# Attention by feature in a two-block layer kernel, and the recurrence's heads normed and turned by halves

## The reference

```python
proj = rms_norm_2(x, g_pre) @ w_in
q_h, f_h, i_h, z_h, q_a, k_a, v_a, z_a = split(proj)
o_h = hgrn2(q_h, f_h, i_h, lb)                       # gated recurrence, 8 heads of 128
o_h = rms_norm_2(o_h, g_head) * silu(z_h)            # per head
o_a = sliding_window_attention(rotary(q_a), rotary(k_a), v_a, sinks)   # 16 heads of 64, window 128
y = concatenate([o_h, o_a * silu(z_a)]) @ w_out
x = x + rms_norm_2(y, g_post)
```

## Time and profile before

| | us |
|---|---|
| median of 3 runs | 1220.43 |
| the runs | 1215.7, 1220.43, 1221.11 |
| the profiled execution | 1216.97 |
| its span, first to last instruction | 1214.8 |
| TensorE busy in it | 1079.9 (89%) |
| VectorE busy | 838.6 (69%) |
| ScalarE busy | 671.2 (55%) |
| GpSimd busy | 71.1 (6%) |
| mean granted TensorE clock | 0.942 |

### The profile page before, as it was taken

The page is one execution under the profiler, slowest core; times in us unless marked ns, Lnnn a source line. Parts: engine busy times, 40 slices in busy tenths (PEclk is TensorE's granted clock), DMA queues, the critical chain, the costliest instruction groups (busy, mean ns, idle before and its releaser), DMA issues.

```text
span 1214.8 us, 16346 instructions
## 1 busy us (share of the span) xinstructions
PE 1079.9 (89%) x6089; PEld 930.8 (77%) x6089; DVE 838.6 (69%) x1516; ACT 671.2 (55%) x1324; POOL 71.1 (6%) x46
## 2 busy tenths in 40 slices
PE   5789798769599999999988899999887889999887
PEld 4668686668588887787877888888766888888766
DVE  5566553456559999999975866686567766587654
ACT  5345374524378988788854487523335378633233
POOL 0100200000010101003000000100101000010100
PEclk9989798879689999999999999999898999999889
DMA  8522124304149999999964322332243322332220
GB/s 333 173 104 105 57 83 162 115 36 174 36 162 398 348 379 365 351 381 369 388 233 161 134 105 104 139 139 105 88 156 130 144 108 105 143 135 105 88 86 35
DMA packets 30034, 211.44 MB, mean 174 GB/s; under 512 B 3328, under 2 KB 3712, under 8 KB 4992
## 3 DMA queue, kind: packets, MB, share of 16 engines
q1 hardware_dynamic: 28368, 205.01, 45.1%
q10 hardware_dynamic: 1584, 5.34, 1.2%
HBM read 209.28 MB, written 1.05 MB: 173 GB/s over the span
## 4 chain that ended last, share of the span: by engine, by line
PE 59%; DVE 21%; ACT 9%; DMA 5%; issue 4%; POOL 2%; SPq 0%; DVEq 0%; POOLq 0%
PE ps L484 15%; PE ps L486 14%; PE ps L485 14%; DVE w_lo L383 9%; DMA ring<-in_panels 5%; PE ps L489 4%; PE ps L925 3%; ACT s_buf L1737 3%; PE ps L633 2%; ACT L1737 2%; POOL stat L395 2%; DVE gates L383 1%; PE ps L691 1%; DVE scr L383 1%; DVE op_lo L383 1%
## 5 line engine op out<-in xcount | busy, mean ns | idle before, releaser
L383 DVE TENSOR_TENSOR w_lo<-ring,w_hi 128x512 fp32r<-128x512 f32 x760 | 488.4, 700 | 201.0 <-ACT w_hi L1690 200.2
L1690 ACT ACTIVATE w_hi<-ring 128x512 fp32r<-128x512 f32 x760 | 424.8, 620 | 249.5 <-PE ps L486 216.2
L484 PE MATMUL ps<-w_hi,op_hi 128*128 128x512 f32 (+2 forms) x928 | 370.5, 399 | 21.6 <-DVE w_lo L383 13.4
L485 PE MATMUL ps<-w_lo,op_hi 128*128 128x512 f32 (+2 forms) x928 | 361.5, 390 | 0.0
L486 PE MATMUL ps<-w_hi,op_lo 128*128 128x512 f32 (+2 forms) x928 | 361.5, 390 | 0.0
L484 PEld LDWEIGHTS ps<-w_hi,op_hi 128*128 128x128 f32 x928 | 177.9, 192 | 63.3 <-DVE w_lo L383 22.2
L486 PEld LDWEIGHTS ps<-w_hi,op_lo 128*128 128x128 f32 x928 | 177.3, 191 | 36.4
L485 PEld LDWEIGHTS ps<-w_lo,op_hi 128*128 128x128 f32 x928 | 177.9, 192 | 32.0
L484 PE MATMUL ps<-op_hi,w_hi 128*128 128x256 f32 x448 | 134.5, 300 | 8.2 <-DVE op_lo L383 8.2
L485 PE MATMUL ps<-op_lo,w_hi 128*128 128x256 f32 x448 | 130.5, 291 | 0.0
L486 PE MATMUL ps<-op_hi,w_lo 128*128 128x256 f32 x448 | 130.2, 291 | 0.0
(11 more groups left out here) (226 smaller groups left out, 1059.1 us busy)
## 6 DMA issues: line engine op xcount, KB each, us to landing
ring<-in_panels SPq DMA_DIRECT2D x194, 1024.0 KB, 6.4
cst<-in_c ACTq DMA_DIRECT2D x1, 1219.0 KB, 5.3
buf_a<-in_pre ACTq DMA_DIRECT2D x2, 512.0 KB, 6.2
keys<-in_post ACTq DMA_DIRECT2D x2, 512.0 KB, 3.6
out<-x_tok SPq DMA_DIRECT2D x2, 512.0 KB, 2.6
cst<-in_c ACTq DMA_DIRECT2D x1, 960.0 KB, 7.0
x_tok<-in_x SPq DMA_DIRECT2D x1, 512.0 KB, 4.7
x_tok<-in_x ACTq DMA_DIRECT2D x1, 512.0 KB, 4.9
```

The source lines that it names most:

```text
L383: return V.tensor_tensor(o, a, b, op)
L484: T.matmul(o, l[0], r[0], start=start, stop=False)
L485: T.matmul(o, l[0], r[1], start=False, stop=False)
L1690: return A.activation(o, a, ACT.Copy, scale=scale)
```

## The change

- `turn` is no longer a transpose. VectorE (`weigh`, new) makes the reciprocals before it, in the sparse attention times the gate, and writes four diagonal matrices, identity times reciprocal. TensorE multiplies the exponentials by them in six fp32 products. The turned probabilities come out already divided.
- `values` has V as the stationary side, in four products with 256 or 128 columns of tokens, so the output is by feature. In the forgetting attention ScalarE and VectorE split it at once into `fox_hi` and `fox_lo`; in the sparse attention VectorE adds the branches; in the second block VectorE multiplies silu(z_a), which is now projected by feature. `up_turns`, `att_turn` and `att_gate` are gone; `up_split` (behind 43) and `att_split` (behind takes 32 and 33 of a layer) split without a turn.
- VectorE runs `scores_out` and `weigh` ahead of the other small work of a take, right behind the feed.
- The projection of z_a moves from takes 26 to 33 to takes 10 to 17 of a layer, the q and f of the recurrence to 18 to 33; the levels from the second on are one take earlier, `cross` is behind 48 and 49.
- `head_norm`, the new `head_scale` and `hg_turn` go by halves of the heads. Eight small products apply inverse root and gate together; the head gain is applied in the split behind the turns.
- In the first block `fox_norms` is behind take 9, `nsa_sides` behind 26, the sparse jobs start one take later, the compression's products use the weighted probabilities, and its weights are loaded one half panel earlier.

```diff
     def weight_halves():
+            if n == 8 and h == 1:
+                out += [(2 * PN_CMP + i, 0, None) for i in range(2)]
             if n == 9 and h == 0:
-                out += [(2 * PN_CMP + i, 0, None) for i in range(2)]
-            if n == 9 and h == 1:
                 out += [(2 * PN_CMP + 2 + i, 0, None) for i in range(2)]
...
     def at_ticks(table, rows):
-        for name, job in (("values", values), ("turn", turn), ("scores", scores)):
+        for name, job in (("weigh", turn), ("values", values), ("turn", turn), ("scores", scores)):
...
-    table.setdefault(b + 33, []).append(("att_gate", l))
+    for a in range(TT):
+        table.setdefault(b + 32 + a, []).append(("att_split", (l, a)))
     for lv in range(LEVELS):
         for j in range(2):
-            table.setdefault(b + L_IH + 2 * lv + j, []).append(("level", (l, lv, j)))
-    table.setdefault(b + 49, []).extend([("cross", (l, 0)), ("cross", (l, 1)), ("att_turn", l)])
...
+            table.setdefault(b + L_IH + 2 * lv + j - (lv > 0), []).append(("level", (l, lv, j)))
+    for j in range(2):
+        for take, name in ((48, "cross"), (50, "hgrn_values"), (51, "head_norm"), (53, "head_scale"), (54, "hg_turn")):
+            table.setdefault(b + take + j, []).append((name, (l, j)))
...
             def turn(job):
-                pe.wait_ge(score_p, job + 1)
+                pe.wait_ge(weighed, job + 1)
...
-                        m = turn128(ps[:, 4 + e, i * P:(i + 1) * P], s_of(job)[:, e * 384 + c:e * 384 + c + P])
+                        m = T.matmul(ps[:, 4 + e, i * P:(i + 1) * P], s_of(job)[:, e * 384 + c:e * 384 + c + P],
+                                     weight_of(job, 1 if i else 0, e), start=True, stop=True)
...
+            def weigh(job):
+                dve.wait_ge(score_p, job + 1)
+                if job >= L1_JOBS:
+                    dv(tt(sm, sm, ex, ALU.add))
+                    settle()
+                dv(V.reciprocal(rec, sm))
+                settle()
...
+                dve.wait_ge(turn_mm, job)
+                for a in range(TT):
+                    for e in range(2):
+                        m = ts(weight_of(job, a, e), ident[:, :], rec[:, 2 * a + e:2 * a + e + 1], None, ALU.mult)
+                m.then_inc(weighed, 1)
...
             def values(job):
+                for kt in range(2):
+                    for e in range(2):
+                        half, cc = slice(e * HD, (e + 1) * HD), c + e * HD
+                        pt = pt_of(job)[:, e * 384:(e + 1) * 384]
+                        m = T.matmul(ps[half, 6, kt * P:S], v3[:, kt, cc:cc + HD], pt[:, kt * S:S + kt * P],
                                      start=kt == 0, stop=kt == 1)
...
+            def head_scale(arg):
...
+                for a in range(TT):
+                    for h in range(4):
+                        m = V.scalar_tensor_tensor(oh[:, a, h, :], oh[:, a, h, :], ss[:, a, h:h + 1], zh[:, a, h, :],
+                                                   ALU.mult, ALU.mult)
+                m.then_inc(hg_done, 1)
...
+            def ahead(t):
+                feed(2 * t + AHEAD)
+                for name, arg in beside.get(t, ()):
+                    if name in ("weigh", "scores_out"):
+                        table[name](arg)
```

More of the change, by code:

```diff
@@ new lines, in dve_program, with up_split, att_split @@
+            cmp_sums, value_sums = [6], (10, 11)
+            def up_split(_):
+                for r in range(PAIRS):
+                    dve.wait_ge(up_hi, r + 1)
+                    o = operand(1024 + r * S, S)
+                    tt(tm(o[1]), z3[:, :, ZNQ + r * P:ZNQ + (r + 1) * P], tm(o[0].bitcast(F32)),
+                       ALU.subtract).then_inc(up_lo, 1)
+            def att_split(arg):
+                l, a = arg
+                for h in range(2):
+                    dve.wait_ge(split_hi, 4 * l + 2 * a + h + 1)
+                    c = ZQA + h * 512
+                    tt(att_lo[:, a, c:c + 512], zb3[:, a, c:c + 512],
+                       att_hi[:, a * D + h * 512:a * D + (h + 1) * 512].bitcast(F32), ALU.subtract).then_inc(split_lo, 1)
@@ L1602, in dve_program @@
                 which, i = divmod(t - T_UP, 4)
-                if i == 0:
-                    for n in range(2):
-                        dve.wait_ge(up_hi, 2 * which + n + 1)
-                        o = operand(1024 * which + n * 512, 512)
-                        tt(o[1], ps[:, n, :], o[0].bitcast(F32), ALU.subtract).then_inc(up_lo, 1)
-                feed(2 * t + AHEAD)
+                ahead(t)
                 b = i % 2
@@ L1746, in turn_out_, with values_out, up_split, att_split @@
                 copy(pt_of(job).rearrange("p (e c) -> p e c", e=2), ps[:, 4:6, 0:384]).then_inc(turn_out, 1)
+            def values_out(job):
+                if job < FOX_JOBS:
+                    act.wait_ge(value_mm, job + 1)
+                    copy(fox_rows(job)[0], ps[:, 6, 0:S]).then_inc(value_hi, 1)
+            def up_split(_):
+                act.wait_ge(cmp_v, 8)
+                for r in range(PAIRS):
+                    act.wait_ge(value_out, 9 + r)
+                    copy(tm(op_hi[:, 1024 + r * S:1024 + (r + 1) * S]),
+                         z3[:, :, ZNQ + r * P:ZNQ + (r + 1) * P]).then_inc(up_hi, 1)
+            def att_split(arg):
+                l, a = arg
+                act.wait_ge(value_out, L1_JOBS + SWA_PAIRS * (l + 1))
+                for h in range(2):
+                    c = ZQA + h * 512
+                    copy(att_hi[:, a * D + h * 512:a * D + (h + 1) * 512], zb3[:, a, c:c + 512]).then_inc(split_hi, 1)
             def compress(step):
@@ L1855, in hgrn_values, with hg_turn @@
                     nc.scalar.dma_start(g_row, pre_in[1].partition_broadcast(P)).then_inc(ld_pre, 16)
-            def back_his(l, half):
-                for b in range(4):
-                    act.wait_ge(back_T, 8 * l + 4 * half + b + 1)
-                    copy(op_hi[:, b * 512:(b + 1) * 512], ps[:, b, :]).then_inc(back_hi, 1)
+            def hg_turn(arg):
+                l, j = arg
+                for b in (2 * j, 2 * j + 1):
+                    act.wait_ge(back_T, 4 * l + b + 1)
+                    copy(op_hi[:, b * 512:(b + 1) * 512], ps[:, b, :], lay_of(l, 0, 1)).then_inc(back_hi, 1)
             def y_squares(l, a):
@@ L1921, in act_program @@
                 which, i = divmod(t - T_UP, 4)
-                if i == 0:
-                    for n in range(2):
-                        act.wait_ge(up_T, 2 * which + n + 1)
-                        c = 1024 * which + n * 512
-                        copy(op_hi[:, c:c + 512], ps[:, n, :]).then_inc(up_hi, 1)
                 feed(2 * t + AHEAD)
```

331 lines of the change are left out of this document (165 added, 166 removed).

## The result

| | us | against before |
|---|---|---|
| before, median of 4 (1215.7 to 1221.34) | 1220.77 | |
| after, median of 4 (1297.2 to 1301.41) | 1299.07 | 1.065, 95% interval 1.062 to 1.069 |
| forecast | 1274, range 1230 to 1308 | |

The change makes the kernel 78 us slower. On the traces, which the rest goes by, it is 83.9 (spans 1298.7 and 1214.8). The direction and the main cost came as forecast; the time is 25 us above the forecast, within the range.

The account below looks back on a forecast made before the run. TensorE, busy 89% of the span, was taken as the bound, so edits elsewhere count only if it waits. Terms 61 + 28 - 33 + 2 + 7 - 8 = +57 us on 1217 gave 1274, range 1230 to 1308.

Parts of the forecast that it names:

- The turn chain, +61: Second-block layers: turn waits for VectorE's diagonal products behind weight pieces, turn doubled; +3.8 us per job, 16 jobs, ends 54 and 74.
- 61 + 2: Turn chain's +61, plus +2 us for projecting the layers' gate by feature, 2.9 against 2.8 us a take, 16 takes.
- The clock, +28: Layers' jobs: idles of about 4.4 us bring half-clock stretches; 1.75 us a job with some spared, ends 0 and 42.
- Second block's end, -33: Recurrence end, both layers: GpSimd gain product, attention turns, head-norm wait and half clock go; 16 us per layer, ends -36 and -27.
- the low end: Second block's end: -27 instead of -33, VectorE 3 us late in each layer for fp32 splits of the attention output.
- Forgetting attention, +7: First block: later turns 0.6 us for three jobs, 2.0 for the first, turns +0.7 each; norms 0; ends -2 and +3.
- +12 + 4 - 5 - 7: Sparse attention: longer chains and turns +12, gelu before exponentials +4, side-turn wait gone -5, compression-weight wait gone -7.
- Up-projections, -18 and +6: First block: turns, splits and their waits go, 50.7 us stretch to about 32.5, -18; new waits lower the clock three times, +6.
- the first (the clock stays up): Layers' jobs: idles of 4.4 us are too short to lower the clock, the +28 falls away, 1246 us; chance 0.17.
- the second (it stays down through each round): Layers' jobs: half clock lasts through each round, costing 5.2 instead of 1.75 us a job, +55, 1329 us; chance 0.05.
- the fourth (half of the 33): Layer tail: halved norm still holds VectorE and attention splits delay the levels, half of the 33 comes, 1290 us; chance 0.08.
- The third: Not slower: layers' turn at most 2.0 us later per job, turn length and clock included, by VectorE's position; 1217 us; chance 0.12.

## Why the prediction was right, and where it was off

- **The turn chain, +61.** Right in place, mechanism and size. VectorE's pieces, forecast at 1.83 us, stand for 1.72; the four products, an estimate of 0.9 between bounds, took 0.88; the turn grew from 0.81 to 1.53 (+0.7). Rounds are 14.6 to 16.4 us and each turn has twelve records, as named. Jobs less the clock's part are 95.4 - 33 = 62 us, for 61 + 2.
- **The clock, +28.** Right, 33 measured. I spared some jobs; none was spared. Here the rule of the Trainium skill (TensorE: Matmul & The Clock Gate, HAM oscillation) was the better guide on how many would pay, all 16, as the trace shows. The price of one that pays, 2.0 to 2.3 us by the earlier trace rows, was right: 2.1 measured.
- **Second block's end, -33.** (Twice its sum of 15.9 is 32, not 33.) The stage's -32.5 looks like a hit and is not: 2.7 us a layer of it are work that the changed kernel does earlier, under the levels. Levels and end together lost 25.9 us. The cross products and attention turns gave 8.4 and 9.0 us for 9.2. The head norm gave 4.8 and 5.1 for 6.7; by halves on the kernel before it gave 6.2 and 6.5. In the changed kernel the second half of the heads is turned one take behind the first, and TensorE waits 1.10 us for it at 940.64. I had named as the low end that VectorE comes 3 us late in each layer for the splits of the attention output. The levels show no such lateness: their only wait is 0.69 us, before 0.49.
- **Forgetting attention, +7.** The stage's +7.7 is near by luck. The head norms, put at 0, cost 1.5 us over takes 12 to 15; the first three jobs cost 6.8 for the 5.3 that they have in the sum; the fourth, 1.9, falls into take 24, the next stage; and takes 0 to 11 were 0.6 shorter.
- **Sparse attention.** My terms up to take 39 are +12 + 4 - 5 - 7 = +4, and 4.4 came, but with one job moved out of the stage and the fourth job of the forgetting attention in it. The wait for the compression's weights went as forecast: the second product has none. A wait that I had not named came in:

```profile
135.62 1.55 PE L683 MATMUL ps<-pt_buf,zin 128*64 128x256 f32 x8 [4.35 <-DVE fox_lo L389]
```

- **Up-projections, -18 and +6: the step that failed.** The stage was to lose 12 us and gained 0.5; without the job that moved in it would have lost 2 to 3. I counted the turns and splits that go, which did go, and one or two waits that stay. What I did not do is to follow VectorE's order where a job's scores and its weighing fall into one take: it then stands for ScalarE's exponentials with the full bank of the values and the gates queued behind it, 6.4 us twice. TensorE's waits in the stage add up to 18.9 us by their brackets, and did so to 18.2 before; its half clock lasted 23.9 us for 27.3. Reordering gave back 5 us of the stage.
- **Output and router.** +3.2 us, not forecast. The edit touches nothing there. The same three waits stand there in both traces (6.18, 2.39 and 5.55 us before, 6.19, 2.39 and 5.71 after), but before, the granted clock came back between the first two and after it did not: 30.7 us at half clock before, 34.1 after. The stage took 61.7 to 67.3 us among kernels in this way. What decides it stays open.

By stages, 4 us in the jobs, 7 in levels and end, 17 in the first block, less 1.5 in the experts, make the 27 us between +57 and +84. Of the rivals, the first (the clock stays up) falls with the 33 us of the filled wait, the second (it stays down through each round) with stretches of 3.4 and 6.8 us in rounds of 14.6 to 16.4, and the fourth (half of the 33) with the 25.9 that came. The third needed a turn at most 2.0 us later, with clock and length; it was 3.0, and 6.0 with them. That it was a matter of VectorE's position was right: with position and order mended and the division done on the rows, TensorE no longer waits for it in the plain rounds.

## What to carry to other kernels

An operation moved in front of a wait costs, besides its own time, what stands queued ahead of it on its engine: four small products of 0.88 us cost 6 us a job here, by their place, by the lower clock behind the longer stop, and by a turn twice as long. When such a chain is mended, read again what is late next after each step; three edits that each moved one instruction group ahead gave 44, 24 and 13 us, and one that only shortened work on TensorE gave its time back as a wait. Take apart a change with two halves: one half here was worth 24 us by itself, beneath a loss of some 100. And where an edit moves work between stages, look at what crosses their borders before a difference is given a cause: here 2.7 us a layer of plain work looked like lateness in one stage and like a gain in the next.

## What the runs showed of the hardware

- TensorE's clock fell behind waits that I had thought too short: with the weighing first, of each layer's eight, 2.58 to 3.06 us long, it fell behind six, and stayed up behind one of 2.58 us in the first layer with the same work around it; behind 4.30 to 4.79 us it fell 16 times in 16. Filling the wait with matmuls that nobody reads kept it at 0.99 over the first layer's jobs and was worth 33 us in the two layers.
- One GpSimd product over two tensors (4.51 us) stretched a pair of VectorE products from 1.29 to 4.68 us; without it they were back at 1.29.
- A diagonal product of 128x128 in fp32 on VectorE takes 0.22 us (four in 0.88), little over half of a 128x256 one (0.406).
